# Down projection of an MLP on one Trainium2 core: twelve of sixteen groups multiplied as six blocks in seven products of halves

## The chip, the cores and the metric

The kernel runs on one core of one Trainium2 chip. The metric is the device time of one execution in microseconds (us). The kernel before took 3367.76 us, the median of three runs (3365.55 to 3372.26).

The engines that the text speaks of are PE (TensorE, matrix multiplication; PEld is its weight load), DVE (VectorE), ACT (ScalarE), POOL (GpSimd) and SP, whose queue issues the DMAs here. Each engine works through its own program in order and waits at semaphores.

## The reference, cut to what matters

Two layers run over 1152 tokens (128 context tokens and 1024 latent ones) of width 1024. Each layer ends with a squared-ReLU MLP of inner width 4096:

```
def sq_relu_ffn(h, w1, w2):
    return jnp.square(jax.nn.relu(h @ w1)) @ w2
```

The change touches the second product, `hidden @ w2`: per layer a 1152 x 4096 matrix times a 4096 x 1024 matrix, in float32. The result is scaled by a norm and a gate and added to the residual in the stage that follows ("the end stage").

## The kernel before, in words

**Precision by three passes.** A float32 operand is split into a high part (ACT copies it with rounding to the matmul's type) and a low part (the operand less its high part, by default on POOL). A product is then three matmuls: high x high, high x low, low x high. So every operand of PE costs one ACT copy and one subtraction, which reads two tensors in SBUF.

**The up projection** (hidden = relu(h @ w1) squared) already works by halves. From the third of 16 groups on (`PLAIN = 2`) each group of 256 inner columns is done as seven products of half-size operands instead of eight (`fast_product`, L1022; sums of weight quarters on DVE in `weight_sums`, L964 to L972; splits in `weight_high` L983 and `weight_low` L987). Its results go to a DRAM tensor `hidden`.

**The down projection** goes over the same 16 groups of 256 inner rows, all of them plainly. The first 14 of each layer are `down_products` (L1044): per group 18 units, nine tiles of 128 tokens times two halves of 512 output columns, and per unit two slices of 128 rows times three passes, so 6 matmuls of 128x512. Each unit goes to one of eight PSUM banks (`DOWN_BANK`). DVE adds the bank to the running sum `yacc` in SBUF (L1234; for group 0 a copy, L1236) and gives it back (`dn_kept`). PE may run eight units ahead of DVE.

The operands of a group come by two DMAs of `hidden` (`hidden_load`, L1256) and one of `w2` (`w2_load`, L1243). ACT makes the high parts (`hidden_high` L1083, 128x2304; `w2_split_high` L1090, 128x2048), POOL the low parts (`hidden_low` L1094, `w2_split_low` L1098), both into two slots each, as soon as the group before last is multiplied. The last two groups belong to the end stage (L1371), in which PE also feeds the norm and the next layer's projections. Nothing is planned by costs: the order on every engine is the order of the program text.

Of the kernel before, what the change touches and what calls it, by code (L numbers as in the profile page):

```python
# [11 lines left out]
F32 = mybir.dt.float32  # L12
# [6 lines left out]
P = 128  # L19
# [54 lines left out]
def trunk(nc, A):  # L74
    st = ExitStack()
    with st:
# [797 lines left out]
        def plain_store(sp, l, g, m, tb):  # L874
# [11 lines left out]
        SUMS_AT = WT0 + 16 * K  # L886
# [3 lines left out]
        s3_lo, s2_hi, s2_lo, s3_hi, s4_hi = (Region(SUMS_AT + n * SUM_SIZE, RAW0)(name, [P, KH, HT], F32R)  # L890
                                             for n, name in enumerate(("s3_lo", "s2_hi", "s2_lo", "s3_hi", "s4_hi")))
# [10 lines left out]
        t_rest = Region(SUMS_AT + 5 * SUM_SIZE, RAW0)  # L902
        t_head = Region(WT0, SUMS_AT)
# [122 lines left out]
        def down_nth(l, g):  # L1026

            return DOWNS * l + 18 * g

        def down_products(pe, l, g):  # L1030
            pe.wait_ge(w2_low, NG * l + g + 1)
            pe.wait_ge(hid_low, NG * l + g + 1)
            for u in range(18):
                n = 18 * g + u
                if n >= 8:
                    pe.wait_ge(dn_kept, down_nth(l, 0) + n - 7)
                elif n == 4:
                    pe.wait_ge(x_kept, len(X_KEPT))
                elif n == 6:
                    pe.wait_ge(yz_kept, 3 * FAST)  # L1040
                w2 = (w2_part, w2_last)[g % 2]
                for m in range(2):
                    for i, (a, b) in enumerate(PASSES):
                        mm = nc.tensor.matmul(psum[:, DOWN_BANK[n % 8], :], H1[:, g % 2, a, m, (u // 2) * P:(u // 2 + 1) * P], w2[b][:, m, (u % 2) * 512:(u % 2 + 1) * 512],  # L1044
                                              start=(m == 0 and i == 0), stop=(m == 1 and i == 2))
# [27 lines left out]

        def hidden_high(act, l, g):
            act.wait_ge(hraw_in[g % 2], 32 * (g // 2 + 1))
            if g == 0:
                act.wait_ge(f_done, step_nth(7, NG - 1))
            elif g == 1:
                act.wait_ge(f_done, step_nth(3, NG - 1))
                act.wait_ge(h_out[1], 32 * (FAST // 2))  # L1080
            else:
                act.wait_ge(dn_sum, down_nth(l, g - 1))
            nc.scalar.activation(as_rows(H1[:, g % 2, 0, :, :]), raw_hidden(g), ACT.Copy).then_inc(hid_high, 1)  # L1083

        def w2_split_high(act, l, g):
            act.wait_ge(w2_in[g % 2], 16 * (NG // 2 * l + g // 2 + 1))
            if g == 1:
                act.wait_ge(yz_kept, 3 * FAST)
                act.wait_ge(h_out[0], 32 * (FAST // 2))
            nc.scalar.activation(WF[:, 1 - g % 2, 0, :], w_raw(g), ACT.Copy).then_inc(w2_high, 1)  # L1090

        def hidden_low(pool, l, g):
            pool.wait_ge(hid_high, NG * l + g + 1)
            nc.gpsimd.tensor_tensor(as_rows(H1[:, g % 2, 1, :, :]), raw_hidden(g), as_rows(H1f[:, g % 2, 0, :, :]), ALU.subtract).then_inc(hid_low, 1)  # L1094

        def w2_split_low(pool, l, g):
            pool.wait_ge(w2_high, NG * l + g + 1)
            nc.gpsimd.tensor_tensor(WF[:, 1 - g % 2, 1, :], w_raw(g), WFf[:, 1 - g % 2, 0, :], ALU.subtract).then_inc(w2_low, 1)  # L1098

        def mlp_scalar(act, l):  # L1100
# [30 lines left out]
            for g in range(PLAIN, NG):  # L1131
                if g > PLAIN:
                    act.wait_ge(yz_kept, yz_nth(0, 1, g - 1))
                keep(6, g, u2_s[:, :])
                for p in (6, 7, 2):
                    weight_high(act, l, p, g + 1)
                if g > PLAIN:
                    act.wait_ge(yz_kept, yz_nth(1, 1, g - 1))
                keep(5, g, u4_s[:, :])
                weight_high(act, l, 5, g + 1)  # L1140
                if g + 1 < NG:
                    act.wait_ge(yz_kept, yz_nth(0, 0, g))
# [9 lines left out]
            for g in range(1, NG):  # L1152
                hidden_high(act, l, g)
                w2_split_high(act, l, g)
            gate_scalar(act, l, 1)

        def mlp_gpsimd(pool, l):
            pool.wait_ge(s_high, S_HIGH[3])
            nc.gpsimd.tensor_tensor(s3_lo[:, :, :], s3_s4[:, :, :], s3_hi[:].bitcast(F32), ALU.subtract).then_inc(s3_low, 1)
            for p, g in STEPS:  # L1160
                weight_low(pool, l, p, g)
            for g in range(NG):
                hidden_low(pool, l, g)
                w2_split_low(pool, l, g)

        def mlp_vector(dve, chain, l):
# [59 lines left out]
            for g in range(DOWN_GROUPS):  # L1226
                if g:
                    dve.wait_ge(dn_kept, down_nth(l, g))
                for u in range(18):
                    n = 18 * g + u  # L1230
                    y, x = yacc[:, u // 2, (u % 2) * 512:(u % 2 + 1) * 512], psum[:, DOWN_BANK[n % 8], :]
                    dve.wait_ge(dn_sum, down_nth(l, 0) + n + 1)
                    if g:
                        tt(y, y, x, add).then_inc(dn_kept, 1)  # L1234
                    else:
                        nc.vector.tensor_copy(y, x).then_inc(dn_kept, 1)  # L1236

        def w2_load(sp, l, g):
            if g < 2:
                sp.wait_ge(f_low, step_nth(4, NG - 2 + g))  # L1240
            else:
                sp.wait_ge(w2_low, NG * l + g - 1)
            sp.dma_start(w_raw(g).rearrange("p (m n) -> p m n", m=2), A["ffn_w2"][l].rearrange("(m p) n -> p m n", p=P)[:, 2 * g:2 * g + 2, :]).then_inc(w2_in[g % 2], 16)  # L1243

        def hidden_load(sp, l, g):
            if g < 2:
                sp.wait_ge(f_done, step_nth(1 + g, NG - 1))
            else:
                sp.wait_ge(hid_low, NG * l + g - 1)
            if g < PLAIN:  # L1250
                for tb in range(3):
                    sp.wait_ge(plain_out[tb], 16 * (plain_nth(l, g, 1) + 1))
            else:
                sp.wait_ge(h_out[g % 2], 32 * (nth_fast(g) // 2 + 1))
# [3 lines left out]
        def mlp_sync(sp, l):  # L1258
# [7 lines left out]
            for g in range(PLAIN, NG):  # L1266
                if g + 2 < NG:
                    raw_load(sp, l, g + 2)
                elif g + 2 == NG:
                    w2_load(sp, l, 0)  # L1270
                else:
                    hidden_load(sp, l, 0)
                    w2_load(sp, l, 1)
                    hidden_load(sp, l, 1)
# [3 lines left out]
            for g in range(2, NG):  # L1278
                hidden_load(sp, l, g)
                w2_load(sp, l, g)  # L1280
                if g == NG - 5:
                    end_ahead(sp, l)
            if l + 1 < LAYERS:
                sp.wait_ge(w2_low, NG * (l + 1))
# [77 lines left out]
        def end_tensor(pe, l):  # L1362
            q = 2

            def down(t, h, g):
# [35 lines left out]
            pe.wait_ge(w2_low, NG * (l + 1) - 1)  # L1401
            pe.wait_ge(hid_low, NG * (l + 1) - 1)
# [4 lines left out]
            pe.wait_ge(w2_low, NG * (l + 1))  # L1407
            pe.wait_ge(hid_low, NG * (l + 1))
# [103 lines left out]
        def end_vector(dve, chain, l):  # L1512
# [45 lines left out]
            dve.wait_ge(hid_low, NG * (l + 1) - 1)  # L1558
# [2180 lines left out]
```

## Time and profile before

| | |
|---|---|
| median of three runs | 3367.76 us |
| the profiled execution's own time | 3366.47 us |
| its span, first to last instruction | 3364.8 us |
| PE busy | 3071.9 us (91%) |
| DVE, ACT, POOL busy | 1999.2, 1181.5, 1213.7 us |
| mean granted clock of TensorE | 0.939 of full speed |
| `down_products`, layer 0 | 1436.14 to 1781.58 us |
| `down_products`, layer 1 | 2948.21 to 3293.69 us |

Times of stages are microseconds from the start of the span. A row of the timeline reads: start, duration, engine, line, operation, output<-inputs, shape, count; in brackets the engine's idle time before it and what ended it. A row of the windows reads: the window, its length, then for PE, PEld, DVE, ACT and POOL the busy time and count, then the granted clock (1.00 is 2.4 GHz, 0.50 is 1.2 GHz), the DMA share and GB/s.

### The profile page before, as it was taken

The page shows a single profiled execution, that of the slowest core. Times are in us where ns is not written, and L with a number is a line of the kernel's source. Part 1 is how long each engine was busy: PE and PEld are TensorE (multiplying, and loading weights), DVE is VectorE, ACT ScalarE, POOL GpSimd, SP SyncE. Part 2 cuts the span into 40 slices and gives each one's busy share as a digit, 9 for nine tenths or more (in the row PEclk, how much of TensorE's full clock was granted, in tenths as well). Part 3 has the DMA queues.
Part 4 walks back from the last instruction along what each step waited for, and adds up shares of the span by engine and source line. Part 5 has one row for each costly group of instructions (what it writes and reads, how often), then busy time and mean ns, then how long its engine had stood idle before and what let it go on. Part 6 is the DMA issues. An engine that isn't in the chain of part 4 may idle for free.

```text
span 3364.8 us, 44682 instructions
## 1 busy us (share of the span) xinstructions
PE 3071.9 (91%) x17804; PEld 2688.8 (80%) x17804; DVE 1999.2 (59%) x2683; ACT 1181.5 (35%) x1884; POOL 1213.7 (36%) x707
## 2 busy tenths in 40 slices
PE   7999878999889899999998899857799899999998
PEld 3888647899778899978886898656678899978886
DVE  3699579555477644455555555477787544455555
ACT  2333233555453332211113476543253323211112
POOL 1466336100033444344341311145443444344341
PEclk9999989999899999999999899966699999999999
DMA  5565544100032232332521332321132232332421
GB/s 199 190 215 195 184 131 128 58 1 1 11 112 80 87 101 94 128 121 92 151 80 51 125 128 70 132 80 43 47 105 83 80 107 92 124 121 98 145 80 57
DMA packets 211326, 347.01 MB, mean 103 GB/s; under 512 B 18696, under 2 KB 110896, under 8 KB 211120
## 3 DMA queue, kind: packets, MB, share of 16 engines
q1 hardware_dynamic: 211120, 344.16, 30.7%
q8 instruction: 142, 2.33, 0.3%
q14 instruction: 64, 0.52, 0.1%
HBM read 259.18 MB, written 84.94 MB: 102 GB/s over the span
## 4 chain that ended last, share of the span: by engine, by line
PE 70%; DVE 14%; POOL 6%; issue 4%; ACT 2%; DMA 1%; SPq 1%; POOLq 1%; DVEq 0%; ACTq 0%
PE psum L1044 21%; PE psum L1022 18%; PE psum L692 6%; PE psum L2198 4%; PE psum L695 3%; DVE ada_acc L298 3%; PE psum L1371 3%; PE psum L2186 2%; PE psum L2193 2%; PE psum L2498 2%; DVE mix_x L2681 1%; PE psum L463 1%; PE psum L2844 1%; DVE mix_v L2694 1%; PE psum L3440 1%
## 5 line engine op out<-in xcount | busy, mean ns | idle before, releaser
L1044 PE MATMUL psum<-WF,H 128*128 128x512 f32 x3024 | 690.9, 391 | 11.2 <-POOL WF L1098 11.2
L1044 PEld LDWEIGHTS psum<-WF,H 128*128 128x128 f32 x3024 | 571.1, 189 | 130.6 <-POOL WF L1098 11.6
L1234 DVE TENSOR_TENSOR yacc<-yacc,psum 128x512 f32<-128x512 f32 x468 | 321.7, 687 | 314.7 <-PE psum L1044 314.7
L1022 PE MATMUL psum<-AT,w_slot 128*128 128x288 f32 x2688 | 365.6, 295 | 0.0
L1022 PEld LDWEIGHTS psum<-AT,w_slot 128*128 128x128 f32 x2688 | 359.4, 188 | 0.0
L1094 POOL TENSOR_TENSOR H<-pass_a,H 128x2304 fp32r<-128x2304 f32 x32 | 165.5, 5172 | 449.5 <-ACT H L1083 449.5
L1022 PE MATMUL psum<-s_hi,w_slot 128*128 128x288 f32 x1344 | 273.6, 298 | 21.7 <-POOL w_slot L987 20.0
L692 PE MATMUL psum<-WT,AT 128*128 128x512 f32 (+1 forms) x1296 | 284.2, 380 | 3.9 <-ACT stage L738 3.9
L1083 ACT ACTIVATE H<-pass_a 128x2304 fp32r<-128x2304 f32 x32 | 68.2, 2131 | 596.8 <-PE psum L1044 573.0
L692 PEld LDWEIGHTS psum<-WT,AT 128*128 128x128 f32 x1296 | 233.2, 192 | 47.8 <-ACT stage L738 4.1
L628 POOL TENSOR_TENSOR WT<-RAW,WT 128x1024 fp32r<-128x1024 f32 (+3 forms) x34 | 114.8, 3401 | 347.2 <-ACT WT L617 347.2
L987 POOL TENSOR_TENSOR w_slot<-RAW,w_slot 128x512 fp32r<-128x512 f32 x112 | 150.8, 1357 | 244.4 <-ACT w_slot L983 244.4
L1022 PEld LDWEIGHTS psum<-s_hi,w_slot 128*128 128x128 f32 x1344 | 219.3, 191 | 22.5 <-POOL w_slot L987 20.4
L1181 DVE SCALAR_TENSOR_TENSOR hid<-hid 128x576 f32<-128x576 f32 x112 | 141.9, 1267 | 118.3 <-ACT hid L1103 115.4
L2498 PE MATMUL psum<-WT,AT 128*128 128x512 f32 x864 | 206.8, 399 | 2.8 <-POOL WT L2632 2.8
L298 DVE SCALAR_TENSOR_TENSOR ada_acc<-ada_raw,silu_c,ada_acc 128x512 f32<-128x512 f32 x126 | 202.5, 1607 | 4.5
L1022 PE MATMUL psum<-s_lo,w_slot 128*128 128x288 f32 x672 | 200.4, 298 | 0.0
L2498 PEld LDWEIGHTS psum<-WT,AT 128*128 128x128 f32 x864 | 164.5, 192 | 38.0 <-POOL WT L2632 3.6
L695 PE MATMUL psum<-AT,WT 128*128 128x384 f32 (+1 forms) x936 | 172.2, 342 | 2.4 <-ACT stage L738 2.4
L695 PEld LDWEIGHTS psum<-AT,WT 128*128 128x128 f32 (+1 forms) x936 | 160.8, 184 | 10.5 <-ACT stage L738 2.7
L987 POOL TENSOR_TENSOR w_slot<-t,w_slot 128x512 fp32r<-128x512 f32 x84 | 127.1, 1514 | 108.3 <-ACT w_slot L983 108.3
L319 POOL TENSOR_TENSOR ada_acc<-ada_acc,ada_scaled 128x512 f32<-128x512 f32 x90 | 137.5, 1527 | 73.4 <-DVE ada_acc L291 61.2
(397 smaller groups left out, 5395.7 us busy)
## 6 DMA issues: line engine op xcount, KB each, us to landing
RAW<-ffn_w SPq DMA_DIRECT2D x64, 1024.0 KB, 6.1
ada_raw<-ada_w SPq DMA_DIRECT2D x18, 2048.0 KB, 8.1
pass_a<-hidden SPq DMA_DIRECT2D x64, 576.0 KB, 5.0
hidden<-hid SPq DMA_DIRECT2D x56, 576.0 KB, 3.3
RAW<-w_in_even SPq DMA_DIRECT2D x5, 2048.0 KB, 8.2
RAW<-w_in_odd SPq DMA_DIRECT2D x5, 2048.0 KB, 8.0
mix_x<-x_all SPq DMA_DIRECT2D x18, 512.0 KB, 3.8
feat_even<-stage SPq DMA_DIRECT2D x36, 256.0 KB, 5.1
```

The costliest lines, as they stand in the source:

```text
L298: nc.vector.scalar_tensor_tensor(acc, w, c, acc, ALU.mult, ALU.add).then_inc(ada_part, 1)
L319: nc.gpsimd.tensor_tensor(acc, acc, ada_scaled[:, k % 2, :], ALU.add).then_inc(ada_added[k % 2], 1)
L692: mm = nc.tensor.matmul(psum[:, s, 0:width], AT[:, a, k, rows_], wt(g, b, width)[:, k, :], start=first, stop=last)
L695: mm = nc.tensor.matmul(psum[0:feats, s, 0:TB], wt(g, a, width)[:, k, cols_], AT[:, b, k, s * TB:(s + 1) * TB], start=first, stop=last)
L987: nc.gpsimd.tensor_tensor(w_slot[p][:, 1, :, :], w_source(p, g), w_slot[p][:].bitcast(F32)[:, 0, :, :], ALU.subtract).then_inc(f_low, 1)
L1022: mm = nc.tensor.matmul(psum[:, bank + b, 0:HB], w_slot[p][:, w, k, :], TOKENS[p][x][:, k, b * HB:(b + 1) * HB], start=(begins and k == 0 ...
L1044: mm = nc.tensor.matmul(psum[:, DOWN_BANK[n % 8], :], H1[:, g % 2, a, m, (u // 2) * P:(u // 2 + 1) * P], w2[b][:, m, (u % 2) * 512:(u % 2 ...
L1094: nc.gpsimd.tensor_tensor(as_rows(H1[:, g % 2, 1, :, :]), raw_hidden(g), as_rows(H1f[:, g % 2, 0, :, :]), ALU.subtract).then_inc(hid_low, 1)
L1181: nc.vector.scalar_tensor_tensor(h, h, 0.0, h, ALU.max, ALU.mult).then_inc(h_ready, 1)
L1234: tt(y, y, x, add).then_inc(dn_kept, 1)
L2198: mm = nc.tensor.matmul(psum[:, 6, 0:HD], probT[:, n % 2, b * P:(b + 1) * P], vK[:, b, 64 * (n % 2):64 * (n % 2) + 64], start=(b == 0), st ...
L2498: mm = nc.tensor.matmul(psum[:, 2 * s + h, :], AT[:, a, k, t * P:(t + 1) * P], wt(8 * l + N_GROUPS + h, b, 512)[:, k, :], start=(k == 0 an ...
```

## The change

Groups 0 to 11 of each layer's down projection become six blocks (`BLOCKS = 6`) of two groups each. In a block, 1024 latent tokens x 512 inner rows x 1024 output columns are cut into halves in all three directions and done with seven products of halves instead of eight. The context tile (128 tokens) is done plainly within the same block, in four quarters. Groups 12 and 13 stay as they were, and so do 14 and 15 in the end stage. The parts:

- `block_load`: per block four loads of 512 KB of `hidden`, two of its context columns in pieces of 64 columns, four of 512 KB of `w2`, each issued when the buffer of the block before is free.
- `block_sums` (DVE): eight sums of 128x1024 from SBUF tensors, four of token quarters and four of weight quarters. Those of block b+1 stand in DVE's program behind the results of products 5 (two), 6 (four in a chain) and 7 (two) of block b.
- `block_high` (ACT): 15 copies of 128x1024 and one of 128x512 per block, into a ring of three slots; a slot is free when the product three places earlier is done.
- `block_low` (POOL): ten subtractions of 128x1024 and one of 128x512. `block_rest` (DVE): the other five, the low weights of products 3 to 7.
- `block_product` (PE): order 1, 2, 0, 3, 4, 5, 6, 7. A product has four units ("pairs" of token tiles and a half of the columns) of 6 matmuls; products 1, 2, 0, 3 also have a context unit of 6, and product 0 is nothing but that. So a block has 32 units. The 28 pairs go round a ring of six PSUM banks (`D_RING`), the context to two further banks.
- `block_keep` (DVE): 28 pairs and two context units per block are added to seven running sums in SBUF (four in `yacc`, three in the token buffer), in the first block copied.
- Only behind the last block the seven sums are merged by seven 128x2048 additions on DVE: one behind product 2, four behind product 6, two behind product 7.
- `end_ahead` (the end stage's early loads) is issued at group 14 in place of group 11, once the first unit of group 12 is kept.

```diff
+        BLOCKS = 6
+        PLAIN_DOWN = 2 * BLOCKS
+        DOWN_BANK = (7, 3, 0, 1, 6, 4, 5, 2)
...
+        D_ORDER = (1, 2, 0, 3, 4, 5, 6, 7)
+        D_RING = (0, 1, 6, 4, 5, 2)
...
+        def block_low(pool, b, p):
...
+            if p:
+                pool.wait_ge(f_high, done - 1)
+                nc.gpsimd.tensor_tensor(d_slot[n % 3][:, 0, 1, :, :], D_TOKENS[p], d_slot_f[n % 3][:, 0, 0, :, :], ALU.subtract).then_inc(f_low, 1)
+            if p in D_REST:
+                return
...
+        def block_rest(dve, b, p):
+            n = 8 * b + D_ORDER.index(p)
+            dve.wait_ge(f_high, len(STEPS) + 16 * b + D_HIGHS[p])
+            nc.vector.tensor_tensor(d_slot[n % 3][:, 1, 1, :, :], D_WEIGHTS[p], d_slot_f[n % 3][:, 1, 0, :, :], ALU.subtract).then_inc(s_low, 1)
...
+        def block_product(pe, l, b, p):
...
+                if q >= 6:
+                    pe.wait_ge(dn_kept, down_nth(l, *pair_unit(q - 6)))
...
+        def block_sums(dve, l, b, part):
...
+            if part == 0:
...
+                tt(s[1], x[0, 1], x[1, 1], add).then_inc(s_ready, 1)
+                tt(t[1], w[0, 1], w[0, 0], sub).then_inc(t_ready, 1)
+            elif part == 1:
...
+                tt(s[2], s[1], x[0, 0], sub).then_inc(s_ready, 1)
+                tt(t[2], w[1, 1], t[1], sub).then_inc(t_ready, 1)
+                tt(s[4], x[1, 0], s[2], sub).then_inc(s_ready, 1)
+                tt(t[4], w[1, 0], t[2], sub).then_inc(t_ready, 1)
+            else:
+                tt(s[3], x[0, 0], x[0, 1], sub).then_inc(s_ready, 1)
+                tt(t[3], w[1, 1], w[0, 1], sub).then_inc(t_ready, 1)
...
+        def block_vector(dve, chain, l, b):
...
+            for p in (1, 2, 3, 4, 5, 6, 7):
...
+                for pair in range(4):
+                    block_keep(dve, l, b, D_FIRST[p] + pair, D_ACC[p][:, pair, :], psum[:, D_RING[q % 6], :])
+                for later in {2: (3, 4), 3: (5,), 4: (6,), 5: (7,)}.get(p, ()):
+                    block_rest(dve, b, later)
+                if b + 1 < BLOCKS:
+                    if p >= 5:
+                        block_sums(dve, l, b + 1, p - 5)
+                elif p in (2, 6, 7):
+                    if p == 2:
+                        chain.mark(tt(y11, y11, d_e1, add))
+                    elif p == 6:
+                        chain.link(tt(y21, y21, d_e1, add))
+                        chain.mark(tt(d_e1, y12, y21, add))
+                        chain.link(tt(y21, y21, d_e4, add))
+                        chain.mark(tt(y12, d_e1, d_e3, add))
+                    else:
+                        chain.link(tt(y21, y21, y22, add))
+                        chain.link(tt(y22, y22, d_e1, add))
...
-            for g in range(DOWN_GROUPS):
+            for b in range(BLOCKS):
+                for p in D_ORDER:
+                    block_product(pe, l, b, p)
+            for g in range(PLAIN_DOWN, NG - 2):
                 down_products(pe, l, g)
```

## Rows read from the trace of the kernel before

**Rows 1.** The chain of waits, the pieces around the down projections (start, us, what).

```profile
1436.14 345.44 PE psum L1044 x1512
...
2948.21 345.48 PE psum L1044 x1512
```

**Rows 2.** Windows of the up and the down projection of layer 0.

```profile
1119.00:1424.00 305.00, 304.15 (x2280) 303.95 (x2278) 130.27 (x147) 87.41 (x149) 129.14 (x95) 0.99 0.32 107
1436.00:1782.00 346.00, 345.43 (x1512) 285.58 (x1512) 173.72 (x253) 55.41 (x29) 136.60 (x29) 0.99 0.33 106
```

**Rows 3.** Timeline: DVE adding units of group 12.

```profile
1735.37 0.69 DVE L1234 TENSOR_TENSOR yacc<-yacc,psum 128x512 f32<-128x512 f32 x1 [0.60 <-PE psum L1044]
1736.73 0.69 DVE L1234 TENSOR_TENSOR yacc<-yacc,psum 128x512 f32<-128x512 f32 x1 [0.67 <-PE psum L1044]
```

**Rows 4.** Groups by line and shape: busy us, mean ns | idle before.

```profile
L1098 POOL TENSOR_TENSOR WF<-RAW,WF 128x2048 fp32r<-128x2048 f32 x32 | 148.3, 4635 | 0.0
L2627 POOL TENSOR_TENSOR AT<-mix_v,AT 128x1024 fp32r<-128x1024 f32 x18 | 43.1, 2394 | 108.1 <-ACT AT L2579 108.1
L2611 ACT ACTIVATE WF<-RAW 128x1024 fp32r<-128x1024 f32 x2 | 2.1, 1054 | 0.0
L1530 DVE TENSOR_TENSOR pass_a<-x_ahead,pass_a 128x1024 f32<-128x1024 f32 x4 | 4.9, 1224 | 0.1
```

**Rows 5.** Timeline: DVE back to back on SBUF tensors while POOL is idle.

```profile
1107.80 0.69 DVE L968 TENSOR_TENSOR RAW<-RAW 128x512 f32<-128x512 f32 x1
1108.41 0.68 DVE L972 TENSOR_TENSOR t<-RAW,t 128x512 f32<-128x512 f32 x1
...
1109.48 2.55 DVE L1203 TENSOR_TENSOR s_s<-s_s,AT 128x2304 f32<-128x2304 f32 x1
1111.95 0.55 DVE L872 TENSOR_TENSOR relu_t<-relu_t 128x384 f32<-128x384 f32 x1
```

**Rows 6.** Timeline: DVE and POOL in the same microseconds; first in group 12.

```profile
1734.92 5.19 POOL L1094 TENSOR_TENSOR H<-pass_a,H 128x2304 fp32r<-128x2304 f32 x1 [14.74 <-ACT H L1083]
...
1425.98 5.14 POOL L1094 TENSOR_TENSOR H<-pass_a,H 128x2304 fp32r<-128x2304 f32 x1 [13.47 <-ACT H L1083]
1428.27 3.47 DVE L1181 SCALAR_TENSOR_TENSOR hid<-hid 128x576 f32<-128x576 f32 x1 [2.80 <-ACT hid L1103]
1431.07 5.02 POOL L1098 TENSOR_TENSOR WF<-RAW,WF 128x2048 fp32r<-128x2048 f32 x1
1432.43 4.27 DVE L1181 SCALAR_TENSOR_TENSOR hid<-hid 128x576 f32<-128x576 f32 x1
...
1101.17 2.55 DVE L1173 TENSOR_TENSOR s_lo<-s_sum,s_hi 128x2304 fp32r<-128x2304 f32 x1
1101.53 3.35 POOL L987 TENSOR_TENSOR w_slot<-t,w_slot 128x512 fp32r<-128x512 f32 x1 [2.02 <-ACT w_slot L983]
1103.64 1.66 DVE L872 TENSOR_TENSOR relu_t<-relu_t 128x384 f32<-128x384 f32 x1
```

**Rows 7.** Windows behind two idle times of PE (clock: third number from the end).

```profile
1436.00:1438.00 2.00, 1.86 (x4) 1.50 (x5) 0.71 (x1) 0.00 (x0) 0.09 (x1) 0.50 0.24 99
1438.00:1444.00 6.00, 6.00 (x21) 4.81 (x20) 2.07 (x3) 3.93 (x2) 1.80 (x1) 0.72 1.00 340
1793.00:1799.00 6.00, 5.50 (x18) 4.47 (x19) 0.00 (x0) 0.00 (x0) 0.44 (x1) 0.72 0.74 254
```

**Rows 8.** Timeline: ACT and SP ahead of the down projection; PE's two restarts.

```profile
1423.23 0.65 ACT L1103 ACTIVATE u_s<-psum 128x576 f32<-128x576 f32 x1 [8.88 <-PE psum L1022]
...
1408.80 4.67 SPq L1277 DMA_DIRECT2D hidden<-hid  x2
...
1436.14 1.22 PE L1044 MATMUL psum<-WF,H 128*128 128x512 f32 x2 [5.56 <-POOL WF L1098]
...
1793.49 5.71 PE L1371 MATMUL psum<-WF,H 128*128 128x512 f32 x18 [6.60 <-POOL WF L1098]
```

**Rows 9.** DMA issues of the page: KB each, median us to landing.

```profile
pass_a<-hidden SPq DMA_DIRECT2D x64, 576.0 KB, 5.0
```

More of the change, by code:

```diff
@@ new lines, in trunk @@
+        d_context = down_a[:, :, 0:KH, 512:HT].rearrange("p h k n -> p k h n")
+        t_front = Region(gate_row_at + 4 * 3 * TB, AT0)
+        context_part = [t_front(f"context_part{hl}", [P, KH, P], F32R) for hl in range(2)]
+        context_halves = lambda a: a.rearrange("p k (h n) -> p k h n", h=2)
+        d_s = {n: down_a[:, i // 2, KH + 2 * (i % 2):KH + 2 * (i % 2) + 2, 0:512] for i, n in enumerate((1, 2, 3, 4))}
+        t_sums = Region(WT0, WT0 + 16 * K)
+        d_t = {n: t_sums(f"d_t{n}", [P, 2, 512])[:, :, :] for n in (1, 2, 3, 4)}
@@ new lines, in down_nth, with plain_down_nth, d_lows, d_rest @@
+        def down_nth(l, b, u):
+            return DOWNS * l + BLOCK_UNITS * b + u + 1
+        def plain_down_nth(l, g):
+            return DOWNS * l + BLOCK_UNITS * BLOCKS + 18 * (g - PLAIN_DOWN)
+        def d_lows(b, p):
+            return len(STEPS) + 11 * b + D_LOWS[p]
+        def d_rest(b, p):
+            return len(S_LOW) + 5 * b + D_REST[p]
+        def d_last_unit(p):
+            return 10 if p == 0 else D_FIRST[p] + 3
+        def d_sums_done(engine, b):
+            engine.wait_ge(s_ready, 4 + 4 * (b + 1))
+            engine.wait_ge(t_ready, 4 * FAST + 4 * (b + 1))
@@ new lines, in block_arrived, with block_load, w2, rows @@
+        def block_arrived(b, p):
+            sets = {1: (raw_in[0], 64, FAST // 2), 2: (raw_in[1], 32, FAST // 2), 0: (hraw_in[0], 32, 0), 3: (hraw_in[1], 32, 0), 4: (hraw_in[1], 32, 0)}
+            s, each, before = sets[p]
+            return s, 16 * before + each * (b + 1)
+        def block_load(sp, l, b):
+            def w2(k, n, s):
+                sp.dma_start(d_weights[k, n], A["ffn_w2"][l].rearrange("(m p) n -> p m n", p=P)[:, 4 * b + 2 * k:4 * b + 2 * k + 2, 512 * n:512 * n + 512]).then_inc(s, 16)
+            def rows(k, cols):
+                return hidden[l][4 * b + 2 * k:4 * b + 2 * k + 2, :, cols].rearrange("m p n -> p m n")
+            def tokens(k, th, s):
+                sp.dma_start(d_tokens[k, th], rows(k, slice(512 * th, 512 * th + 512))).then_inc(s, 16)
+            if b == 0:
+                for tb in range(3):
+                    sp.wait_ge(plain_out[tb], 16 * PLAIN_UNITS * (l + 1))
+                sp.wait_ge(f_done, step_nth(1, NG - 1))
+                sp.wait_ge(f_low, step_nth(4, NG - 2))
+            else:
+                for s in range(2):
+                    sp.wait_ge(h_out[s], 32 * (b))
+                d_sums_done(sp, b - 1)
+            for p, k, th, n, s in ((1, 0, 0, 0, raw_in[0]), (2, 1, 0, 0, raw_in[1]), (0, 0, 1, 1, hraw_in[0]), (4, 1, 1, 1, hraw_in[1])):
+                if b:
+                    sp.wait_ge(f_low, d_lows(b - 1, p))
+                    if p == 4:
+                        sp.wait_ge(s_low, d_rest(b - 1, 3))
+                elif n:
+                    sp.wait_ge(f_low, step_nth(4, NG - 1))
+                tokens(k, th, s)
+                if p == 1:
+                    for h in range(2):
+                        sp.dma_start(down_a[:, h, 0:KH, 512:HT], hidden[l][4 * b:4 * b + 4, :, 1024 + 64 * h:1024 + 64 * h + 64].rearrange("m p n -> p m n")).then_inc(s, 16)
+                w2(k, n, s)
@@ new lines, in block_rest, with pair_unit @@
+        def block_rest(dve, b, p):
+            n = 8 * b + D_ORDER.index(p)
+            dve.wait_ge(f_high, len(STEPS) + 16 * b + D_HIGHS[p])
+            nc.vector.tensor_tensor(d_slot[n % 3][:, 1, 1, :, :], D_WEIGHTS[p], d_slot_f[n % 3][:, 1, 0, :, :], ALU.subtract).then_inc(s_low, 1)
+        def pair_unit(q):
+            b, i = q // 28, q % 28
+            p = [p for p in D_ORDER if p][i // 4]
+            return b, D_FIRST[p] + i % 4
+        def block_product(pe, l, b, p):
+            n = 8 * b + D_ORDER.index(p)
+            slot = d_slot[n % 3]
+            pe.wait_ge(f_low, d_lows(b, p))
+            if p in D_REST:
+                pe.wait_ge(s_low, d_rest(b, p))
+            if p in D_QUARTER:
+                k_half, n_half = D_QUARTER[p]
+                begins = k_half == 0
+                if begins and b:
+                    pe.wait_ge(dn_kept, down_nth(l, b - 1, (4, 9)[n_half]))
+                elif begins and n_half:
+                    pe.wait_ge(yz_kept, 3 * FAST)
+                for k in range(2):
+                    for i, (x, w) in enumerate(PASSES):
+                        mm = nc.tensor.matmul(psum[:, CONTEXT_BANK[n_half], :], context_part[x][:, 2 * k_half + k, :], slot[:, 1, w, k, :],
+                                              start=(begins and k == 0 and i == 0), stop=(k == 1 and i == 2), skip_group_check=not begins)
+                if not begins:
+                    mm.then_inc(dn_sum, 1)
+            if p == 0:
+                return
+            for pair in range(4):
+                q = 28 * b + D_FIRST[p] - (0, 0, 1, 2, 2, 2, 2, 2)[p] + pair
+                if q >= 6:
+                    pe.wait_ge(dn_kept, down_nth(l, *pair_unit(q - 6)))
+                elif q == 3:
+                    pe.wait_ge(x_kept, len(X_KEPT))
+                elif q == 5:
+                    pe.wait_ge(yz_kept, 3 * FAST)
+                for k in range(2):
+                    for i, (x, w) in enumerate(PASSES):
+                        mm = nc.tensor.matmul(psum[:, D_RING[q % 6], :], slot[:, 0, x, k, pair * P:(pair + 1) * P], slot[:, 1, w, k, :],
+                                              start=(k == 0 and i == 0), stop=(k == 1 and i == 2))
+                mm.then_inc(dn_sum, 1)
@@ L1151, in mlp_scalar @@
                     weight_high(act, l, p, g + 1)
-            for g in range(1, NG):
+            for b in range(BLOCKS):
+                for p in D_ORDER:
+                    if (b, p) != (0, 1):
+                        block_high(act, l, b, p)
+            for g in range(PLAIN_DOWN, NG):
                 hidden_high(act, l, g)
@@ L1161, in mlp_gpsimd @@
                 weight_low(pool, l, p, g)
-            for g in range(NG):
+            for b in range(BLOCKS):
+                for p in D_ORDER:
+                    block_low(pool, b, p)
+            for g in range(PLAIN_DOWN, NG):
                 hidden_low(pool, l, g)
```

228 lines of the change are left out of this document (150 added, 78 removed).

## The prediction

> **What bounds the kernel now.** I read the chain of waits first. Of the two down projections it holds one piece of 345.44 us and one of 345.48 us, both PE, with 1512 matmuls each [rows 1]: PE waits for nobody there. The windows say the same and show the room beside it: in 346 us PE is busy for 345.43, DVE for 173.72, POOL for 136.60, ACT for 55.41 [rows 2]. DVE's additions start 1.36 us apart, so one unit of 6 matmuls takes PE 1.36 us, and DVE idles for about 0.67 us in each [rows 3]. A group of 18 units is 24.5 us, two groups are 49.0 us. In this stage a matmul that goes away is time won, as long as DVE, POOL and ACT keep under PE. Whether they do is the whole question.
>
> **What goes.** A block has 32 units in place of 36: 4 x 1.36 = 5.4 us less, 43.5 us in place of 49.0. With 12 blocks that would be 65 us, the ceiling of the gain.
>
> **What comes on the other engines, per block.** DVE: 30 results from PSUM. One lasts 0.69 us [rows 3]; back to back I take 0.61 from start to start, as the operation of 0.69 and 512 columns shows in [rows 5]: 18.3 us. 13 operations of 128x1024 with both inputs in SBUF: the starts of [rows 5] are 0.61 us apart for 512 columns and 2.47 for 2304, which gives 1.14 us for 1024 and 2.2 for 2048; the row with 1224 ns [rows 4] agrees, as durations include some 0.08 us of overlap. 13 x 1.14 = 14.8. Together 33.1 us of 43.5. POOL: 10 of 2394 ns [rows 4], 2.37 from start to start, and one of 512 columns; the line through 2.39 at 1024 and 5.14 at 2304 columns [rows 4, 6] gives it 1.28: 25 us. ACT: 15 x 1.05 [rows 4] plus 0.6, 16 us. Each engine alone fits. The context copy has runs of 64 columns, which no row shows; its price on POOL lies between 1.28 and the 2.37 of twice its size. I take 1.28, as the elements are what the other rows count by; the other end would make each block 1 us longer.
>
> **But DVE and POOL don't fit together.** In [rows 6] the squaring L1181 of 576 columns takes 3.47 and 4.27 us, where [rows 5] give 576 columns some 0.7. The first one ends 0.6 us after POOL's H does, and POOL's next operation, begun at 1431.07, is 5.02 us long where it needs 4.6 [rows 4]: DVE was let in between, and POOL waited for it. The last three rows of the group show it with the parts changed: POOL (3.35 us for 1.28) waits until 1103.7 for DVE's 2304-column subtraction, then DVE's next one (1.66 for 0.55 [rows 5]) waits for POOL. So an operation of DVE with two inputs in SBUF and one of POOL exclude each other and take turns. Additions out of PSUM don't: they keep their 0.69 us under a POOL operation [rows 3, 6]. The 13 operations and POOL's 11 need 14.8 + 25 = 39.8 us of exclusive time in 43.5 us, and the program puts them into the same moments: POOL's heaviest stretch (products 1, 2, 0 of the next block) starts when product 5 ends, which is where DVE's eight sums stand.
>
> The Trainium skill, "SBUF — State Buffer", section "Who interferes with whom", says this of the shared ports: a VectorE instruction with two SBUF inputs contends with a GpSimd instruction that reads SBUF, and the one that issues second is fully blocked. The page names no turns. If DVE had to wait out POOL's whole queue, the first sum below would start some 9 us later and the four of product 6 much earlier in POOL's pause; the end of the stall moves by about 1 us per block, some 10 us in all, so the sum below hardly depends on it.
>
> **The schedule, t = 0 at PE's end of product 5.** ACT's and POOL's work for product 1 (free slot) starts at once. DVE: last result 0.1 to 0.7, low weights of 7 to 1.8. POOL context to 3.1, DVE sum to 4.2, POOL tokens to 6.6, DVE sum to 7.75, POOL weights to 10.1. DVE adds product 6's four results from 7.75 to 10.2. POOL tokens of 2 to 12.5, DVE sum 13.6, POOL weights 16.0, DVE sum 17.1, POOL weights of 0 to 19.5, DVE's last two of the chain 20.6 and 21.8. Only then come product 7's results: the first bank is back at 22.4. PE meanwhile: product 6 to 5.4, two pairs of 7 to 8.2, two more to 11.1, context and two pairs of product 1 to 15.2. The ring of six banks is now full, and PE waits 7.2 us for the bank at 22.4. Product 1 ends at 25.1, where a free run would have it at 17.7. The rest of the block costs 26.4 (19 units x 1.36, and 0.5 for low weights of 3). One block: 51.5 us. Seven products take 2.5 us more than the eight did.
>
> **The first block.** SP is free of the store at about 1413.5 [rows 8]; ten loads of 0.5 to 0.6 us issue and 5.0 landing [rows 9] are there by about 1425. ACT begins after 1423.23 + 0.65 [rows 8]; with the turns of L1181, product 1's low parts are ready at 1432.1 where PE now starts at 1436.14: 4.0 us won. DVE does all eight sums ahead of its first result, in turns with POOL until 1451.3; PE has filled six banks by 1442.9 and waits 9.0 us, then 3.4 for the low weights of product 3. Block 0: 56.1 us.
>
> **Behind the last block.** DVE merges 128x2048, 2.2 us each, in turns with POOL's plain splits for groups 12 and 13 (5.1 and 4.6 us [rows 6, 4]). The four behind product 6 end 20 us after product 7. Group 12's first unit waits 3.8 us for its weights; its fifth needs the bank of product 7's first result, which DVE takes only behind the merges: 11.4 us; the ninth 1.4 more. So 16.6 us. `end_ahead` and the loads behind it keep some 25 us of cover; the next block's last load is issued 27 us before its sums, so they cost nothing unless landing takes over five times [rows 9].
>
> **Sum per layer, profiled execution, full clock.** Before: groups 0 to 13 end at 1436.14 + 345.44 = 1781.6. After: start 1432.1, block 0 56.1, blocks 1 to 4 4 x 51.5 = 206.1, block 5 51.3, wait 3.8, groups 12 and 13 49.0 + 12.8: 1811.2. That is 29.6 us later. **The clock:** behind PE's idle 5.56 us before 1436.14 the granted clock is 0.50 (1.2 GHz) and averages 0.72 over the 6 us after 1438, which is half speed for 5.4 us in all; behind the 6.60 us before 1793.49 it is half speed for 3.4 us [rows 7, 8]. That costs 2.7 and 1.7 us. The waits of 7.2 us in blocks 1 to 5 and those at both ends are of that length: 0 to 14.6 us per layer; I take half, 7.4. The old start's own loss (2.7) is inside the 345.44. So 37 us per layer, 74 for both. 3366.47 + 74 = 3440.5; the median shown is 1.3 above the profiled execution: 3442.
>
> **Rivals.**
> 1. *The seven products run free.* If DVE's sums mostly met an idle POOL, PE would set the pace: start 1430.7, blocks 44.0 to 46, end at 1746.5 to 1747.6, 35 us less per layer: 3298. For it: the up projection runs just this scheme with PE at 304.15 of 305 us [rows 2]. Against: there DVE and POOL are busy for 130 and 129 of 305 us, here 36 and 25 of 43.5, and the turns are seen in that very stage. It decides where DVE's wait per block falls under about 6 us; my schedule has some 13, 10.8 of it in the list above. Chance 0.11.
> 2. *Milder collisions.* Semaphore order or POOL's idle gaps let three or four sums through unhindered: blocks of 49 to 50.5, the merges as above, no clock fall: +8 to +23 us per layer, 3384 to 3414. Chance 0.22. Two layers with blocks at 47.5 and the merges unchanged would be no change; chance 0.05.
> 3. *Loads in pieces of 256 bytes and 2 KB.* If a block's loads took over 30 us, block_sums would hold DVE with results queued behind it: 55 to 58 us per block, +55 us per layer, 3478 and more. Chance 0.06.
>
> **How the numbers follow.** My forecast (turns, stall at product 1 in every block) has 0.56. What a measurement of this kernel can tell from no change is about 0.2%, 6.7 us. Faster by more: rival 1 and a little of 2, 0.12. Within: 0.05. Slower: 0.83. The range from 3380 to 3475 leaves out rival 1, no change and rival 3. Within the forecast the time runs from 3427 (full clock) to 3456 (every stall loses 2.7).
>
> **What would show it.** Right: PE busy falls by 288 x 0.227 = 65 us yet the stage grows; PE idle of about 7 us per block in front of product 1's third pair, released by DVE; durations of block_sums' and the merges' operations of 2.3 to 7 us for 1.2 and 2.2 of work; POOL's 2.4 growing to 3.5; a gap of about 11 us in group 12; clock under 1 behind these. Wrong: blocks 44 us apart, durations at 1.22, or idle released by DMA.

## The result, and the profile after

The changed kernel takes 3447.2 us (median of 4; 3446.32 to 3448.71) beside 3368.95 us for the kernel before on the same chip. The ratio is 1.0233 (95% interval 1.022 to 1.0245): 2.3% slower, with 288 matmuls fewer. The forecast was 3442 us.

The chain of waits, layer 0, from the end of the up projection on (start, us, what), to be held against [rows 1]:

```profile
1432.39 3.43 DVE down_a L1214
1435.82 3.35 DVE d_t L1215
1439.16 3.34 DVE down_a L1219
...
1592.56 3.31 DVE down_a L1219
1595.86 3.32 DVE d_t L1221
1599.27 3.12 issue
1604.25 5.22 PE psum L1196 x12
...
1749.29 3.77 DVE yacc L1260
1753.08 6.50 DVE down_a L1261
1759.59 7.14 DVE yacc L1262
1766.75 6.47 DVE yacc L1263
1773.87 46.54 PE psum L1280 x192
```

Where one piece of 345.44 us of PE stood, PE's work now alternates with DVE's sums (L1214 to L1229) and, behind the last block, its merges (L1260 to L1263). Group 13 ends at 1773.87 + 46.54 = 1820.4, 38.8 us later than before. In layer 1 the down projection costs 38.5 us more. The spans differ by 3445.7 - 3364.8 = 80.9 us, so some 3.6 us lie outside the two down projections. PE is busy for 3047.0 us in place of 3071.9: 24.9 us less, though 288 matmuls are gone.

The windows of four blocks (between the restarts of PE in blocks 1 and 5) and of the hand-over to the plain groups, columns as in [rows 2]:

```profile
1497.50:1711.90 214.40, 186.77 (x768) 149.69 (x768) 183.06 (x174) 62.61 (x64) 126.32 (x44) 0.93 0.26 84
1749.00:1821.00 72.00, 57.23 (x238) 46.12 (x237) 54.90 (x47) 8.12 (x5) 31.83 (x6) 0.91 0.43 128
```

A block takes 214.4 / 4 = 53.6 us where two plain groups took 49.0. PE idles 6.9 us in each and is busy for 46.7, which is 2.8 us more than the same 192 matmuls take at full clock (43.9 in a run below). DVE is busy for 85% of the time, but much of this "busy" is waiting inside an instruction. The groups of instructions show it (busy us, mean ns):

```profile
L1148 POOL TENSOR_TENSOR d_slot<-down_a,d_slot 128x1024 fp32r<-128x1024 f32 x84 | 234.9, 2796 | 234.4 <-ACT d_slot L1137 234.4
L1152 POOL TENSOR_TENSOR d_slot<-RAW,d_slot 128x1024 fp32r<-128x1024 f32 x36 | 119.5, 3334 | 0.0
...
L1215 DVE TENSOR_TENSOR d_t<-RAW 128x1024 f32<-128x1024 f32 x12 | 41.0, 3418 | 0.0
L1219 DVE TENSOR_TENSOR down_a<-down_a 128x1024 f32<-128x1024 f32 x12 | 40.8, 3396 | 0.0
...
L1225 DVE TENSOR_TENSOR d_t<-RAW,d_t 128x1024 f32<-128x1024 f32 x12 | 14.5, 1212 | 0.0
L1262 DVE TENSOR_TENSOR yacc<-yacc,down_a 128x2048 f32<-128x2048 f32 x2 | 14.4, 7206 | 0.0
```

Equal sums of 128x1024 take 1.21 us (L1225, when POOL is done) or 3.4 us. POOL's subtraction of the same size is 2.39 us alone [rows 4] and 3.3 when DVE has its turn. No idle time stands in front of DVE's rows: looked at by idle time alone, the wait is invisible.

The timeline of DVE around one stall (start, us, engine, line):

```profile
1583.36 1.22 DVE L1157 TENSOR_TENSOR d_slot<-d_t,d_slot 128x1024 fp32r<-128x1024 f32 x1
1584.50 2.33 DVE L1214 TENSOR_TENSOR down_a<-down_a 128x1024 f32<-128x1024 f32 x1
1586.75 3.42 DVE L1215 TENSOR_TENSOR d_t<-RAW 128x1024 f32<-128x1024 f32 x1
1590.09 2.47 DVE L1234 TENSOR_TENSOR yacc<-yacc,psum 128x512 f32<-128x512 f32 x4
1592.48 3.39 DVE L1219 TENSOR_TENSOR down_a<-down_a 128x1024 f32<-128x1024 f32 x1
1595.79 3.40 DVE L1221 TENSOR_TENSOR d_t<-RAW,d_t 128x1024 f32<-128x1024 f32 x1
1599.11 3.35 DVE L1223 TENSOR_TENSOR down_a<-down_a 128x1024 f32<-128x1024 f32 x1
1602.39 1.21 DVE L1225 TENSOR_TENSOR d_t<-RAW,d_t 128x1024 f32<-128x1024 f32 x1
1603.52 2.47 DVE L1234 TENSOR_TENSOR yacc<-yacc,psum 128x512 f32<-128x512 f32 x4
```

POOL in the same stretch:

```profile
1585.70 3.38 POOL L1148 TENSOR_TENSOR d_slot<-down_a,d_slot 128x1024 fp32r<-128x1024 f32 x1
1589.05 3.38 POOL L1152 TENSOR_TENSOR d_slot<-RAW,d_slot 128x1024 fp32r<-128x1024 f32 x1
1592.38 2.40 POOL L1148 TENSOR_TENSOR d_slot<-down_a,d_slot 128x1024 fp32r<-128x1024 f32 x1
1594.74 6.64 POOL L1152 TENSOR_TENSOR d_slot<-RAW,d_slot 128x1024 fp32r<-128x1024 f32 x2
```

POOL's operation begun at 1592.38 ends at 1594.78. The DVE sum begun at 1592.48 ends at 1595.87, some 1.1 us later, which is its own work. POOL's next pair then needs 6.64 us for 4.8 of work. Both have their next operation at hand, and one of each is served in turn.

Product 6's results are added at 1590.1, product 7's at 1603.5, some 13 us apart, where PE makes a product's four in 5.4. PE's own rows in the same stretch name the releaser:

```profile
1604.25 5.22 PE L1196 MATMUL psum<-d_slot 128*128 128x512 f32 x12 [6.30 <-DVE yacc L1234]
...
1757.49 5.73 PE L1280 MATMUL psum<-WF,H 128*128 128x512 f32 x24 [3.52 <-POOL WF L1341]
1773.87 11.39 PE L1280 MATMUL psum<-WF,H 128*128 128x512 f32 x37 [10.65 <-DVE yacc L1234]
```

### The profile page after: what moved, and what is told of

It is laid out like the page before. It is cut to its first block, busy times and chain, and to the rows that moved or that the text cites. A ratio compares the mean times of both kernels' runs of the same rounds, so it can differ in the third digit from the quotient of the medians.

```text
span 3445.7 us, 44652 instructions
## 1 busy us (share of the span) xinstructions
PE 3047.0 (88%) x17516; PEld 2650.8 (77%) x17516; DVE 2305.2 (67%) x2781; ACT 1275.4 (37%) x2028; POOL 1368.8 (40%) x791
## 3 DMA queue, kind: packets, MB, share of 16 engines
q8 instruction: 140, 2.29, 0.3%
## 4 chain that ended last, share of the span: by engine, by line
PE 63%; DVE 22%; issue 6%; POOL 6%; ACT 2%; DMA 1%; POOLq 0%; SPq 0%; DVEq 0%; ACTq 0%
PE psum L1024 18%; PE psum L1196 9%; PE psum L692 5%; PE psum L2443 4%; PE psum L695 3%; DVE ada_acc L298 3%; PE psum L1616 3%; PE psum L1280 3%; PE psum L2431 2%; PE psum L2438 2%; PE psum L2743 2%; DVE mix_x L2926 1%; PE psum L463 1%; DVE down_a L1219 1%; DVE d_t L1221 1%
## 5 line engine op out<-in xcount | busy, mean ns | idle before, releaser
L1196 PE MATMUL psum<-d_slot 128*128 128x512 f32 x2016 | 493.2, 405 | 78.6 <-DVE yacc L1234 50.3
L1196 PEld LDWEIGHTS psum<-d_slot 128*128 128x128 f32 x2016 | 393.5, 196 | 171.5 <-DVE yacc L1234 56.5
L1148 POOL TENSOR_TENSOR d_slot<-down_a,d_slot 128x1024 fp32r<-128x1024 f32 x84 | 234.9, 2796 | 234.4 <-ACT d_slot L1137 234.4
L1137 ACT ACTIVATE d_slot<-down_a 128x1024 fp32r<-128x1024 f32 x84 | 89.0, 1059 | 357.9 <-PE psum L1196 341.9
L1430 DVE SCALAR_TENSOR_TENSOR hid<-hid 128x576 f32<-128x576 f32 x112 | 132.0, 1178 | 116.2 <-ACT hid L1346 113.3
L2443 PEld LDWEIGHTS psum<-vK,probT 128*128 128x128 f32 x1280 | 147.7, 192 | 14.2 <-ACT probT L2508 13.0
```

What stands on the lines that cost most here:

```text
L1148: nc.gpsimd.tensor_tensor(d_slot[n % 3][:, 0, 1, :, :], D_TOKENS[p], d_slot_f[n % 3][:, 0, 0, :, :], ALU.subtract).then_inc(f_low, 1)
L1196: mm = nc.tensor.matmul(psum[:, D_RING[q % 6], :], slot[:, 0, x, k, pair * P:(pair + 1) * P], slot[:, 1, w, k, :], start=(k == 0 and i == ...
L1430: nc.vector.scalar_tensor_tensor(h, h, 0.0, h, ALU.max, ALU.mult).then_inc(h_ready, 1)
L2443: mm = nc.tensor.matmul(psum[:, 6, 0:HD], probT[:, n % 2, b * P:(b + 1) * P], vK[:, b, 64 * (n % 2):64 * (n % 2) + 64], start=(b == 0), st ...
```

## The experiments

Theory T: DVE's operations with two SBUF inputs and POOL's operations (those that read SBUF, as e9 will narrow it) exclude each other and take turns; DVE's results stand behind the lengthened ones; the ring of six PSUM banks runs full. Rivals: DVE's queue alone, POOL's load alone, or loads. All ran against the kernel before on the same chip; times are medians. "Block" is the spacing of the same PE event in successive blocks of layer 0.

| run | us | ratio to before (95%) | block, us |
|---|---|---|---|
| after | 3447.2 | 1.0233 (1.022 to 1.0245) | 53.6 |
| e1_no_merges | 3416.5 | 1.0135 (1.0118 to 1.0152) | 53.7 |
| e2_pool_only_writes | 3336.2 | 0.9898 (0.9884 to 0.9913) | 44.55 |
| e3_pool_in_halves | 3376.3 | 1.0019 (1.001 to 1.0028) | 47.05 |
| e4_sums_spread | 3413.2 | 1.0125 (1.011 to 1.014) | 49.5 |
| e5_merges_apart | 3426.8 | 1.0167 (1.0152 to 1.0182) | 53.6 |
| e6_halves_spread_merges | 3352.0 | 0.9941 (0.9926 to 0.9956) | 45.4 |
| e7_halves_late_sums | 3319.3 | 0.9849 (0.9832 to 0.9865) | 43.7 |
| e8_pool_copies | 3339.4 | 0.9907 (0.9892 to 0.9922) | 44.55 |
| e9_pool_long_writes | 3338.4 | 0.9907 (0.989 to 0.9923) | 44.55 |
| e10_late_sums_only | 3356.5 | 0.9961 (0.9947 to 0.9976) | 45.95 |

**e2: POOL writes without reading.**

```diff
-                nc.gpsimd.tensor_tensor(d_slot[n % 3][:, 0, 1, :, :], D_TOKENS[p], d_slot_f[n % 3][:, 0, 0, :, :], ALU.subtract).then_inc(f_low, 1)
+                nc.gpsimd.memset(d_slot_f[n % 3][:, 0, 1, :, :], 0.0).then_inc(f_low, 1)
...
```

The cut lines do the same for the weights and the context.

> The changed kernel with POOL's subtractions inside the blocks put as memsets of the same tensors (the low parts are zeros, the subtraction is left out): POOL still writes 128x1024 each time but reads nothing. DVE's program is untouched. Theory T: DVE's sums and low weights are back at about 1.22 us each, the wait before the third pair of product 1 goes from 6.3 us to under 1, a block takes 44 to 45 us, block 0 about 47 to 50; the merges still meet the plain splits. 50 to 60 us less per layer: 3327 to 3347 us, faster than the kernel before. Rival R (it is the number and the place of DVE's eight sums in front of results, whatever POOL does): DVE's durations may fall, but the ring still runs full: blocks of 50 us or more, 3400 or more.

Measured 3336.2 us, within T's range. The wait at product 1 is gone, though DVE's program is the same: its number and order of sums alone don't fill the ring. But a memset is also shorter than a subtraction, so this run alone leaves "POOL is done sooner" standing.

**e8: POOL copies, one SBUF input.**

```diff
...
+                nc.gpsimd.tensor_copy(d_slot[n % 3][:, 0, 1, :, :], D_TOKENS[p]).then_inc(f_low, 1)
...
```

> The changed kernel with POOL's subtractions in the blocks put as copies of the raw operand (one SBUF input in place of two; the low parts are not low parts, the subtraction is left out). Beside the run with memsets it asks whether POOL's reading is what excludes DVE. Theory T: a POOL operation that reads SBUF takes turns with DVE's two-input ones, a writing one doesn't (1.215 us each in the memset run). So DVE's sums are longer than 1.22 us by up to one POOL copy, and blocks lie between the 44.55 us of the memsets and the 53.5 us of the subtractions, by the copy's duration. Rival (only an operation with two inputs on POOL excludes DVE, or only a long one): DVE's sums stay at 1.22 us and the time is that of the memset run, 3336 us.

Half a miss. The timeline of one stretch:

```profile
1558.88 2.03 POOL L1148 CAST d_slot<-down_a 128x1024 fp32r<-128x1024 f32 x1
1559.93 2.05 DVE L1215 TENSOR_TENSOR d_t<-RAW 128x1024 f32<-128x1024 f32 x1
...
1563.19 1.05 POOL L1148 CAST d_slot<-down_a 128x1024 fp32r<-128x1024 f32 x1 [0.31 <-ACT d_slot L1137]
...
1566.23 1.21 DVE L1221 TENSOR_TENSOR d_t<-RAW,d_t 128x1024 f32<-128x1024 f32 x1
```

Exclusion is there (2.05 for 1.21 on DVE, 2.03 for 1.05 on POOL), so the rival's mechanism is wrong. Yet blocks stay at 44.55 us and the time is the rival's, 3339.4: turns of one microsecond fit into the ring. So exclusion alone doesn't fill the ring; POOL's operations must also be long. T's estimate, in which blocks grow with the copy's duration, was wrong here.

**e9: POOL as long as before, but writing only** (three memsets in a row, each waiting for the one before).

```diff
...
+            for _ in range(2):
+                nc.gpsimd.memset(dst, 0.0).then_inc(pad, 1)
+                padded[0] += 1
+                pool.wait_ge(pad, padded[0])
+            return nc.gpsimd.memset(dst, 0.0)
...
```

> The changed kernel with each of POOL's 128x1024 subtractions in the blocks put as three memsets of the same tensor one after the other (the low parts are zeros, the subtraction is left out). A memset took 0.955 us, so POOL is busy about as long as with the subtractions (some 3 us in place of 2.4), but it reads nothing. It parts two things that the single memset left together: POOL not excluding DVE, and POOL being done sooner. Theory T (exclusion by reading is the cause): DVE's sums stay at 1.22 us, blocks of 44.6 to 45.5 us, 3335 to 3350 us. Rival (POOL's load is the cause: the splits come too late or the engines meet for time, not for the port): blocks of 50 us or more, 3400 and more.

Measured 3338.4 us. The groups and the window of four blocks:

```profile
L1144 POOL MEMSET d_slot<- 128x1024 f32 x240 | 229.4, 956 | 151.0 <-ACT d_slot L1139 143.0 <-ACT d_slot L1140 1.1
L1147 POOL MEMSET d_slot<- 128x1024 f32 x120 | 114.7, 956 | 6.9
...
L1223 DVE TENSOR_TENSOR down_a<-down_a 128x1024 f32<-128x1024 f32 x12 | 14.6, 1220 | 0.0
L1224 DVE TENSOR_TENSOR d_t<-RAW 128x1024 f32<-128x1024 f32 x12 | 14.6, 1219 | 0.0
...
1494.50:1672.70 178.20, 175.75 (x769) 143.85 (x769) 137.30 (x172) 62.67 (x65) 115.88 (x125) 1.00 0.25 83
```

POOL is busy for 344 us on the low parts, about as long as the changed kernel's 354, and DVE's sums take 1.22 us throughout. Compare L1214 and L1215 of the changed kernel, 2.5 and 3.4 us, which these two lines are. So neither POOL's load nor DVE's queue fills the ring: the exclusion by POOL's reading operations does, when they are as long as the subtractions. PE's 769 matmuls take 175.75 us, which gives the 43.9 per block at full clock used above.

**e3: the same work in shorter turns.**

```diff
...
+                for k in range(2):
+                    ins = nc.gpsimd.tensor_tensor(d_slot[n % 3][:, 0, 1, k, :], D_TOKENS[p][:, k, :], d_slot_f[n % 3][:, 0, 0, k, :], ALU.subtract)
+                ins.then_inc(f_low, 1)
...
```

The weights are cut in two likewise, the context operation stays whole.

> The changed kernel with each of POOL's 128x1024 subtractions in the blocks as two of 128x512: the same work, in shorter turns. Theory T: DVE waits up to 1.3 us per turn in place of 2.4, so the sums take about 2.4 in place of 3.4 us; a block takes 48 to 50 us in place of 53.5: 22 to 27 us less per layer, 3393 to 3405 us. Rival R (POOL's sheer load or DVE's): 10 more POOL instructions per block cost something and win nothing: 3447 to 3465 us.

Measured 3376.3 us: more gain than T foretold, outside its range; R is wrong. In PE's rows the wait at product 1 has shrunk from 6.3 to 1.75 us, and the 12 matmuls behind it run at a granted clock of 1.00 (3.03 us in place of 5.22):

```profile
1541.43 3.03 PE L1200 MATMUL psum<-d_slot 128*128 128x512 f32 x12 [1.75 <-DVE yacc L1238]
```

A block is 6.6 us shorter. Windows of four blocks put 4.4 of them down to PE's idle time, inside the 3.5 to 5.5 that T gave the whole block, and 2.2 to PE's busy time. T did not name the clock that comes back.

**e4 and e10: the same work in other places.** e4 puts one sum at a time between results; e10 keeps POOL whole and puts the sums where POOL has little to do (those of block b+1 behind results (5, 0), (6, 0), (6, 3) and (2, 0) of product and pair, the last one already in block b+1). The places in e10:

```diff
...
+        SPREAD = {(2, 0): [(0, 'rest', 3), (0, 't', 4), (0, 's', 3), (0, 't', 3)], (2, 3): [(0, 'rest', 4)], (3, 3): [(0, 'rest', 5)], (4, 3): [(0, 'rest', 6)], (5, 0): [(1, 's', 1), (1, 't', 1)], (5, 3): [(0, 'rest', 7)], (6, 0): [(1, 's', 2)], (6, 3): [(1, 's', 4), (1, 't', 2)]}
...
```

> The changed kernel with the eight sums of DVE spread one by one between the results of products 5, 6, 7 and, in the next block, 1 and 2, and the low weights of product 4 behind a result of product 3. Work and sizes are the same. Theory T: the number of turns that DVE waits for hardly falls, the ring just runs full later and more evenly: blocks about 52 us, 4 to 8 us less per layer, 3431 to 3439. Rival R (place in the queue is all): a result never waits for more than one sum, the waits at product 1 go, blocks of 46 us or less: 3375 or less.

> The changed kernel with the sums at the places of the fastest version so far (two behind the first result of product 5, one behind the first of product 6, two behind its last, three behind the first result of product 2 of their own block), POOL's operations whole and the merges where the change has them. Correct. Theory T: fewer turns meet in front of results of products 6 and 7, the ring covers them: blocks 45.5 to 46.5 us without a clock fall, the wait in group 12 stays at 9 to 11 us: 3350 to 3365 us. Rival (halving POOL's operations does most of it): blocks of 48 us or more, 3380 and more.

e4 took 3413.2 us, between the two ranges and inside neither: blocks of 49.5 for T's 52. Place counts for more than T said, though not for all. The wait at product 1 is gone and another one stands at product 3, for the low weights, and the granted clock falls to 0.50 behind it as well (2.90 us for 6 matmuls, 1.63 in the changed kernel):

```profile
1554.58 2.90 PE L1180 MATMUL psum<-d_slot,context_part 128*128 128x512 f32 x6 [3.61 <-DVE d_slot L1157]
```

e10 took 3356.5 us as T had it: faster than before by 0.4% with nothing moved but DVE's sums and low weights.

**e1 and e5: the merges.** e1 leaves them out; e5 moves them:

```diff
                     if p == 2:
                         chain.mark(tt(y11, y11, d_e1, add))
+                        chain.link(tt(y21, y21, d_e1, add))
                     elif p == 6:
...
+                        chain.link(tt(d_e1, y12, y21, add))
                     else:
...
+                        chain.link(tt(y12, d_e1, d_e3, add))
...
+                    if n == 8:
+                        last_merges(dve, chain)
```

`last_merges` holds the other three.

> The changed kernel without its seven 128x2048 merges behind the last block of each layer (they are left out, so the sums stay apart). Theory T (operations of DVE with two SBUF inputs and operations of POOL take turns, and the merges stand ahead of product 7's results): the PE wait of 10.65 us in group 12 goes, the one of 3.5 us at its start shrinks to about 1, and a clock fall less: 13 to 17 us per layer, 3413 to 3421 us for 3447. The blocks keep 53.5 us. Rival R (the waits at the hand-over come from loads or from POOL's splits of groups 12 and 13 alone): under 4 us per layer, 3439 or more.

> The changed kernel with its seven merges per layer in other places: two behind product 2, one behind product 6, one behind product 7, three behind the eighth unit of group 12. The same work, correct. Theory T (PE's 10.65 us in group 12 are product 7's results behind four merges that take turns with POOL's plain splits): the first of these results waits for one merge only, the 10.65 us go, at most one wait of a few us comes behind the eighth unit: 8 to 12 us less per layer, 3423 to 3431 us. Rival (the merges' time is lost wherever they stand): 3443 to 3449.

Both within T's ranges: 3416.5 and 3426.8 us. In e1 the wait at group 12's start is 1.22 us in place of 3.52 and the one of 10.65 is gone. So the merges cost (3447.2 - 3416.5) / 2 = 15 us per layer, and their place 10.

**e6 and e7: put together.** Halves, spread sums and merges apart; in e7 the sums are where e10 has them.

> POOL in halves, the sums spread as in the run with spread sums, the merges apart: all three edits of order and size at once, correct. Theory T, by laying out the turns: blocks 45 to 46 us, the wait in group 12 gone, 95 to 105 us less than the changed kernel: 3340 to 3355 us, faster than before by 0.4 to 0.9%. Rival (each edit removes the same waits, so they don't add up): not under the 3376 us of the halves alone.

> As the run before, with other places for the sums: the first two of the next block behind the first result of product 5, one behind the first of product 6, two behind its last, the last three behind the first result of product 2 of their own block, where POOL has little to do. Correct. Theory T: PE has no wait over 0.6 us inside a block, blocks 43.6 to 44.5 us, the start 1432 to 1434 and the wait at group 12 about 3.5 us: 3310 to 3330 us, 1.1 to 1.7% faster than before. If more turns meet than laid out: 3330 to 3355.

3352.0 and 3319.3 us, both as T had it. e7 beats both kernels, by 1.5% and 3.7%. The window of its blocks from the last wait of block 0 to the first of block 5:

```profile
1476.00:1682.00 206.00, 205.09 (x900) 168.30 (x898) 178.34 (x201) 72.11 (x74) 152.05 (x98) 1.00 0.29 97
```

PE is busy for 205.09 of 206 us at full clock, with DVE at 87% and POOL at 74%. The single gains don't add up: halves 71, places (e10) 91, merges 20 make 182 us, e7 has 128. They remove the same waits, and PE's own work is the floor inside the blocks. With the stalls gone, loads begin to show: in layer 0 of e7 DVE idles for `w2` loads four times, 9.7 us in all, and the longest of these waits, 3.9 us in front of a sum at 1468.08, is followed by a PE wait of 1.93 us.

## Why the prediction was right

**The mechanism, by its steps.** *Exclusion in turns* was read off rows of another stage [rows 6] and held: sums of 3.4 us, POOL's 2.39 grown to 3.3, results out of PSUM untouched (L1234, 681 ns in the groups of the changed kernel, as [rows 3] had it). The prediction also weighed that DVE might have to wait out POOL's whole queue; the rows of POOL above show one operation of each in turn instead. *The schedule of a block* put product 6's results at 7.75 us and product 7's at 21.8 behind the end of product 5; the timeline has them 13.4 us apart, forecast 14.05. *The full ring*: a wait of 7.2 us in front of product 1's third pair, measured 6.3, released by DVE. *Low weights of 3*: 0.5, measured 0.61. *The first block*: PE starts at 1431.86 (1432.1), waits 7.88 (9.0), and the later 3.4 is 0.62. *The hand-over*: 3.52 and 10.65 us (3.8 and 11.4); the 1.4 at the ninth unit didn't come. *Loads* cost nothing: no wait of PE or DVE in the blocks of the changed kernel names a DMA. One sign that was to show the forecast right did not: PE's busy time was to fall by 65 us and fell by 24.9, as the matmuls behind each stall run slower.

**A term that was mis-sized.** The clock. The forecast took 1.7 to 2.7 us per stall and of their sum only half, 7.4 us per layer. Its upper end, 14.6 us, isn't the sum that it is said to be: five blocks and two ends at 2.7 make 18.9. Windows of the changed kernel around one stall:

```profile
1600.00:1604.00 4.00, 0.00 (x0) 0.00 (x0) 4.00 (x3) 0.00 (x0) 1.38 (x1) 0.77 0.00 0
1604.00:1610.00 6.00, 5.75 (x15) 4.55 (x16) 6.00 (x10) 0.49 (x1) 0.00 (x0) 0.58 0.09 7
1610.00:1613.00 3.00, 3.00 (x15) 2.46 (x14) 2.03 (x4) 1.51 (x2) 2.35 (x1) 1.00 1.00 289
```

By single microseconds the granted clock is 1.00 until 1602, 4 us into the wait, 0.50 (1.2 GHz) from 1603 to 1609, and 1.00 (2.4 GHz) again from 1610 on. Set against the matmuls of e9 and e1 at full clock (43.94 us per block, 49.27 for groups 12 and 13), PE's busy time is longer by 2.9 us in block 0 and up to the first restart of block 1 (50.91 us for 210 matmuls), by 11.0 in the four blocks above, by 1.6 in the rest of block 5 (41.45 for 174) and by 3.0 in groups 12 and 13 (52.26 for 216). That is some 18.5 us in layer 0, where the forecast had 7.4 per layer. A few tenths of it are the restarts themselves.

Against that the terms at full clock were too high: 29.6 us per layer forecast, while 38.8 less 18.5 leaves about 20. The largest differences are block 0 (the 3.4 us wait for the low weights of product 3 was 0.62), blocks 1 to 4 (50.8 us at full clock for 51.5) and the hand-over. The two errors, about +11 and -9 us per layer, nearly cancel. That the total came so close (74 us forecast, 80.9 measured in the spans) is in part luck: the mechanism and its waits were right, the split between waiting and clock was not.

The length of a wait alone doesn't tell what the clock does. At the start of group 12 the changed kernel waits 3.52 us, the clock stays at 1.00 and 24 matmuls take 5.73 us; in e2 PE waits 3.22 us there, the clock falls to 0.50 and the same 24 take 7.40.

**The rivals.** The free run (0.11) fails by e9's contrast: it describes what happens without exclusion, and would have been 3336 to 3338 rather than 3298, mostly since the merges stay (15 us per layer by e1). Milder collisions (0.22) would have left blocks of 49 to 50.5 us without a clock fall; they take 53.6 at a mean clock of 0.93. It was not far off: at full clock they would take 50.8. Of the four sums in front of product 7's results the first three are at 3.4 us, and the fourth is at 1.2, as the forecast's own list had it. Slow loads (0.06) are excluded by the missing DMA waits. DVE's sums stay at 1.22 us under POOL's memsets (e9) and reach 2.05 under its copies (e8). By the Trainium skill, page "SBUF — State Buffer", section "Who interferes with whom", only GpSimd operations that read SBUF stand against such sums; these two runs agree.

**What stays open.** It is not shown where the 3.6 us outside the down projections come from, nor why e4's blocks are 2.5 us shorter than laid out.

## What to carry to other kernels

Before work is moved from PE to DVE, add up the exclusive time of DVE's two-input SBUF operations and POOL's, and look at which moments they share. Each engine alone had room in the forecast's sum (76% of a block on DVE, 58% on POOL); the order of the operations took it away. Even 39.8 us of exclusive time per block of 43.5 isn't too much as such: e7 does about that work in 43.7 us, with POOL's operations in halves and DVE's sums elsewhere. When a POOL operation must stand beside such sums, cut it into shorter ones, place the sums where POOL is idle, and never put long ones in front of results that PSUM banks wait for. A ring of banks covers DVE's delays up to its length (here six banks of 1.36 us of PE's work each, 8 us by estimate); what goes beyond stops PE, and behind a stop of 6 us PE paid again, with 1.6 to 2.9 us of slower matmuls.

## What the runs showed of the hardware that was not expected

- On 128x1024 float32 POOL takes 2.39 us for a subtraction [rows 4], 1.05 for a converting copy (e8) and 0.956 for a memset (e9).
- POOL's memset never lengthened DVE's two-input operations (1.22 us, 96 sums in e9), its copy did (up to 2.05, e8).
- A wait of 3.2 us was followed by a clock of 0.50 (e2), one of 3.5 us in the same place was not (changed kernel).
- In turns, a 2048-column addition of DVE between POOL's operations of 5.1 and 4.6 us took 6.5 to 7.2 us for 2.29 of its own (L1261 to L1263; the first merge, begun while a POOL operation was nearly done, 3.8). Both engines kept strict alternation through the four.
